# V rows gathered 8 tokens by 16 picks at a time and summed with 32-column weight blocks

## What is computed

```python
def block_fn(hb):                       # 128 tokens, four times
    q = (hb @ peer_wq).reshape(B, Q_BLOCK, PEER_HEADS, 2, PEER_HALF)
    s = jnp.einsum('bqhpd,hpnd->bqhpn', q, peer_subkeys).astype(jnp.float32)
    vals, idx = lax.top_k(s, PEER_TOPK)
    ...
    top_s, pos = lax.top_k(combo, PEER_TOPK)
    expert = jnp.take_along_axis(ids, pos, axis=-1)        # 128 tokens x 8 heads x 16 picks
    g = jax.nn.softmax(top_s, axis=-1).astype(hb.dtype)
    u_sel = peer_u[expert]
    a = jax.nn.gelu(jnp.einsum('bqhkd,bqd->bqhk', u_sel, hb))
    v_sel = peer_v[expert]
    return jnp.einsum('bqhk,bqhkd->bqd', g * a, v_sel)
```

## Time and profile before

| what | value |
|---|---|
| device time, median of 3 runs | 3902.87 us (3900.05 to 3913.13) |
| span of the profiled execution, first to last instruction | 3781.4 us |
| what lies around the span, by the median | 121.5 us |
| retrieval, first gather issued to last sum | 514 us to 1884 us of the span |
| gathers | 512 of U, 512 of V, 512 KB each |

### The profile page before, as it was taken

How to read it: one execution, slowest core, us unless ns; L and a number is a source line. 1 busy time by engine, 2 the same in 40 slices (tenths; PEclk the granted TensorE clock), 3 DMA queues, 4 the chain that set the end, 5 groups by cost and what they waited for, 6 DMA issues and landing times. The chain is left out here.

```text
span 3781.4 us, 35208 instructions
## 1 busy us (share of the span) xinstructions
PE 3188.5 (84%) x11752; PEld 1996.0 (53%) x11752; DVE 2418.9 (64%) x4629; ACT 1404.0 (37%) x2228; POOL 1168.3 (31%) x1095
## 2 busy tenths in 40 slices
PE   8988798887777777777788988997799999598878
PEld 4655543332222222222366876875688888465556
DVE  4866457666766776677576446445688888644444
ACT  2324312222222222222243323333588888534443
POOL 0000047777777777777600000000122222000000
PEclk9988799999999999999998988998899999799888
DMA  8322069999999999999932210134799999521101
GB/s 274 109 84 78 24 241 400 397 380 404 407 404 374 407 407 408 408 403 400 357 109 56 79 38 14 51 89 156 267 367 376 370 372 373 179 62 45 28 28 56
DMA packets 420694, 896.23 MB, mean 237 GB/s; under 512 B 37793, under 2 KB 178593, under 8 KB 419874
## 3 DMA queue, kind: packets, MB, share of 16 engines
q0 software_dynamic: 157728, 549.55, 37.1%
q1 hardware_dynamic: 262786, 344.41, 26.9%
HBM read 891.73 MB, written 27.27 MB: 243 GB/s over the span
## 5 line engine op out<-in xcount | busy, mean ns | idle before, releaser
L268 PE MATMUL peer_acc<-peer_vbuf,peer_diag 128*128 128x512 f32 x2016 | 981.3, 613 | 295.6 <-DMA peer_vbuf<-in_peer_v,peer_experts 209.9
L441 DVE CUSTOM_DVE_ANT_0 peer_junk<-peer_ubuf,firsts_h 128x1024 f32<-128x1024 f32 x512 | 626.6, 1225 | 385.3 <-DMA peer_ubuf<-in_peer_u,peer_experts 347.7
L268 PEld LDWEIGHTS peer_acc<-peer_vbuf,peer_diag 128*128 128x128 f32 x2016 | 351.3, 191 | 914.5 <-issue 472.3
L208 POOL DMA_INDIRECT peer_ubuf<-in_peer_u,peer_experts x512 | 526.5, 1028 | 672.7 <-DVE peer_experts L412 513.6
L219 POOL DMA_INDIRECT peer_vbuf<-in_peer_v,peer_experts x512 | 517.7, 1011 | 156.1 <-issue 120.1
L326 ACT ACTIVATE peer_diag<-all_consts,peer_weights 128x128 f32<-128x128 f32 x504 | 191.9, 398 | 800.5 <-PE peer_acc L268 730.6
L3029 DVE TENSOR_TENSOR slotted_low<-slotted_raw,slotted_high 128x2048 fp32r<-128x2048 f32 x192 | 434.1, 2288 | 66.0 <-ACT slotted_high L2978 66.0
L2978 ACT ACTIVATE slotted_high<-slotted_raw 128x2048 fp32r<-128x2048 f32 x192 | 365.5, 1920 | 63.6 <-PE slotted_h L2935 51.3
L2802 POOL MEMSET slotted_xg<- 128x4096 f32 x1 | 3.5, 3512 | 748.4 <-POOLq L60 748.4
L2935 PE MATMUL slotted_h<-slotted_high,slotted_xT_high 128*128 128x512 f32 x512 | 205.1, 401 | 6.2 <-DVE slotted_low L3029 4.1
L2935 PE MATMUL slotted_h<-slotted_high,slotted_xT_low 128*128 128x512 f32 x512 | 201.6, 394 | 0.0
(11 more groups left out here) (748 smaller groups left out, 5811.0 us busy)
## 6 DMA issues: line engine op xcount, KB each, us to landing
slotted_raw<-in_moe_w SPq DMA_DIRECT2D x192, 1024.0 KB, 8.4
mixers_raw<-in_w_in SPq DMA_DIRECT2D x56, 512.0 KB, 3.8
firsts_ada_raw<-in_w_ada SPq DMA_DIRECT2D x64, 256.0 KB, 2.7
third_raw<-in_w_in SPq DMA_DIRECT2D x30, 512.0 KB, 3.7
firsts_raw<-in_w_in SPq DMA_DIRECT2D x28, 512.0 KB, 4.1
firsts_ada_first<-in_w_ada SPq DMA_DIRECT2D x8, 1024.0 KB, 13.3
ffn_w_raw<-in_peer_wq SPq DMA_DIRECT2D x16, 512.0 KB, 7.5
peer_ubuf<-in_peer_u,peer_experts POOLq DMA_INDIRECT x512, 6.9
```

The lines of the kernel that those rows point to most:

```text
L208: pool.indirect_dma_start(ubuf[:, n % R, :], None, A["peer_u"], bass.IndirectOffsetOnAxis(ap=experts[:, t, m:m + 1], axis=0))\
L268: mm = nc.tensor.matmul(acc[t % 2][j][:, :], diag[:, q % 4, :], vbuf[:, n % R, j * BANK:(j + 1) * BANK], start=(m == 0), stop=(m == E - 1 ...
L441: nc.vector.tensor_tensor_reduce(junk[:, n % 2, :], ubuf[:, n % R, :], h2[:, t, :], 1.0, 0.0, ALU.mult, ALU.add, act_in[:, t, m:m + 1]).th ...
```

## The change

The rows of V are fetched in another grouping. Before, one gather held pick i of all 128 tokens. Now one gather holds all 16 picks of 8 tokens: partition 16 j + k is pick k of token 8 c + j, for the column c of a table `v_rows` of row numbers. Sixteen gathers a head, as before, and the same 2048 rows.

- **DVE** writes the picks of a head 8 times side by side (`ids`, 128 x 128). **PE** turns them (`turn_picks`, a matmul with the identity, in the middle of the V sums of the head before). DVE then masks and sums the turned picks to `v_rows` (`rows_of_v`: three operations, at the end of each head's pass), and POOL's first V gather of the head waits for that (`v_chosen`).
- The weights go the same way: `weigh` writes them 8 times, PE turns them (`turn_weights`), and `spread` on DVE (after dot 2 of the next head) makes of them 16 blocks of 32 columns, `spread_w`, in one operation.
- **PE** adds two gathers at a time (`add_rows`): for each a matmul of 128 x 32 weights by 512 columns into one 32-row quarter of the PSUM bank; gathers n and n+1 go to different quarters. As many matmuls as before.
- ACT's diagonals are gone. The dot product writes its products over `ubuf`, not into `junk`. The last head is summed by PE alone. One of four score banks becomes the bank for turning; a small table `own_rows` is loaded.

```diff
                 def gather_v(n):
-                    t, m = place(n)
-                    i = n - R - (G - 1) * PT
-                    if i >= 0 and i % 2:
-                        pool.wait_ge(v_summed, i // 2 + 1)
-                    elif n >= R:
-                        pool.wait_ge(added, n - R + 1 if i < 0 else n - R + 1 - i // 2)
+                    g, i = divmod(n, PT)
+                    if i == 0:
+                        pool.wait_ge(v_chosen, g + 1)
+                    if n >= R:
+                        pool.wait_ge(added, n - R + 1)
                     pool.indirect_dma_start(vbuf[:, n % R, :], None, A["peer_v"],
-                                            bass.IndirectOffsetOnAxis(ap=experts[:, t, m:m + 1], axis=0))\
+                                            bass.IndirectOffsetOnAxis(ap=v_rows[:, g % 2, column_of(i):column_of(i) + 1], axis=0))\
                         .then_inc(v_in[n % R], 16)
...
+                def turn_picks(g):
+                    pe.wait_ge(chosen, g + 1)
+                    if g >= 2:
+                        pe.wait_ge(v_chosen, g - 1)
+                    nc.tensor.matmul(turn_bank[:, tile(g % 2)], ids[:, g % 2, :], C["ident"], start=True, stop=True)\
+                      .then_inc(picks_turned, 1)
...
+                def add_rows(n0):
+                    g, i0 = divmod(n0, PT)
+                    t, h = divmod(g, PH)
+                    if i0 == 0:
+                        pe.wait_ge(weights_spread, g + 1)
+                    for n in (n0, n0 + 1):
+                        pe.wait_ge(v_in[n % R], 16 * (n // R + 1))
                     for j in range(2):
-                        mm = nc.tensor.matmul(acc[t % 2][j][:, :], diag[:, q % 4, :], vbuf[:, n % R, j * BANK:(j + 1) * BANK],
-                                              start=(m == 0), stop=(m == E - 1 or n == G * PT - 2))
-                    mm.then_inc(added, 1)
+                        for n in (n0, n0 + 1):
+                            i = n % PT
+                            rows32 = slice(32 * quarter_of(i), 32 * quarter_of(i) + 32)
+                            mm = nc.tensor.matmul(acc[t % 2][j][rows32, :], spread_w[:, g % 2, column_of(i), :],
+                                                  vbuf[:, n % R, j * BANK:(j + 1) * BANK],
+                                                  start=(h == 0 and i < 4), stop=(h == PH - 1 and i >= PT - 4))
+                            if j == 1:
+                                mm.then_inc(added, 1)
...
+                def rows_of_v(g):
+                    dve.wait_ge(picks_turned, g + 1)
+                    if g == 0:
+                        dve.wait_ge(own_in, 16)
+                    chain(nc.vector.tensor_tensor(picked[:, :, :], turn_bank[:, tile(g % 2)].rearrange("p (i j) -> p i j", i=PT),
+                                                  own8.unsqueeze(1).broadcast_to([P, PT, 8]), ALU.mult))
+                    chain(nc.vector.reduce_sum(v_rows_f[:, :], picked[:, :, :], AX))
+                    if g >= 2:
+                        dve.wait_ge(v_in[R - 1], 16 * (PT // R) * (g - 1))
+                    nc.vector.tensor_copy(v_rows[:, g % 2, :], v_rows_f[:, :]).then_inc(v_chosen, 1)
+
+                def spread(g):
+                    dve.wait_ge(weights_turned, g + 1)
+                    if g >= 2:
+                        dve.wait_ge(added, PT * (g - 1))
+                    nc.vector.tensor_tensor(
+                        spread_w[:, g % 2].rearrange("p (q r) c -> p q r c", q=4),
+                        turn_bank[:, tile(2 + g % 2)].rearrange("p (q c) -> p q c", q=4).unsqueeze(2).broadcast_to([P, 4, 4, 32]),
+                        own32.rearrange("p (r c) -> p r c", r=4).unsqueeze(1).broadcast_to([P, 4, 4, 32]), ALU.mult)\
+                      .then_inc(weights_spread, 1)
...
                         dot(g * PT + i)
                         if g and i == 0:
                             weigh(g - 1)
+                        if g and i == 2:
+                            spread(g - 1)
...
                     finish(coming)
+                    rows_of_v(g)
...
                 weigh(G - 1)
-                last_closed()
+                spread(G - 1)
+                collect(NT - 1)
+                dve.wait_ge(stored, 2 * NT)
+                finish(opened(NT - 1))
```

More of the change, by code:

```diff
@@ L160, in retrieval @@
         vbuf = st.sb("vbuf", [P, R, D])
-        junk = st.sb("junk", [P, 2, D])
         act_in = st.sb("act_in", [P, NT, E])
-        diag = st.sb("diag", [P, 4, P])
-        banks = [st.ps(f"s{i}") for i in range(4)]
+        v_rows, picked = st.sb("v_rows", [P, 2, PT], U32), st.sb("picked", [P, PT, 8])
+        own = st.sb("own", [P, 8 + P])
+        own8, own32 = own[:, 0:8], own[:, 8:8 + P]
+        v_rows_f, spread_w = st.sb("v_rows_f", [P, PT]), st.sb("spread_w", [P, 2, PT, 32])
+        score_banks, turn_bank = [st.ps(f"s{i}") for i in range(3)], st.ps("turn")
         acc = [[st.ps(f"acc{i}{j}") for j in range(2)] for i in range(2)]
@@ L172, in retrieval, with score_bank, quarter_of, column_of @@
         dotted, gelued, softened, weighed = st.sem("dotted"), st.sem("gelued"), st.sem("softened"), st.sem("weighed")
-        diagonal, added, stored, gate_in = st.sem("diagonal"), st.sem("added"), st.sem("stored"), st.sem("gate_in")
-        v_summed = st.sem("v_summed")
+        added, stored, gate_in = st.sem("added"), st.sem("stored"), st.sem("gate_in")
+        picks_turned, v_chosen, weights_turned, weights_spread = (st.sem(n) for n in ("picks_turned", "v_chosen", "weights_turned",
+                                                                                     "weights_spread"))
+        own_in = st.sem("own_in")
         def place(n):
             return n // E, n % E
[L179 to L183, removed]
+        def score_bank(q):
+            return score_banks[q % 3]
+        def quarter_of(i):
+            return i % 4
+        def column_of(i):
+            return 4 * (i % 4) + i // 4
+        def eight_times(rows):
+            return rows.unsqueeze(1).broadcast_to([P, 8, PT])
         def head(g):
@@ L198, in _ @@
                         sp.dma_start(skT[:, :, :], A["subkeys_T"]).then_inc(sk_in, 16)
+                        sp.dma_start(own[:, :], A["own_rows"]).then_inc(own_in, 16)
                 sp.wait_ge(scored, PH + 4 * (NT - 1))
@@ L279, in _ @@
                     per = len(steps) // KD
-                    for i in range(PT):
-                        add_row(h * PT + i)
-                        for step in steps[i * per:(i + 1) * per]:
+                    turn_weights(h)
+                    for i in range(0, PT, 2):
+                        add_rows(h * PT + i)
+                        if i == PT // 2:
+                            turn_picks(h + 1)
+                        for step in steps[i * per:(i + 2) * per]:
                             product(*step)
@@ L290, in _ @@
                         pe.wait_ge(stored, 2 * (t - 1))
[L291 to L294, removed]
+                    for g in range(t * PH, (t + 1) * PH):
+                        turn_weights(g)
+                        for i in range(0, PT, 2):
+                            add_rows(g * PT + i)
+                            if i == PT // 2 and g + 1 < G:
+                                turn_picks(g + 1)
+                        if g == t * PH + PH // 2 and t + 1 < NT:
                             later_scores(t + 1)
@@ L315, in gelu @@
                       .then_inc(gelued, 1)
[L317 to L327, removed]
                 def query_moved(m):
```

79 lines of the change are left out of this document (34 added, 45 removed).

## The result

The changed kernel takes 4000.04 us in the median of 4 runs (3991.27 to 4011.77). The kernel before, timed with it, took 3904.03 us (3900.05 to 3913.13), so the ratio is **1.0239, 95% interval 1.022 to 1.0258**: 96 us slower, where +110 was predicted. Timed again with the first group of experiments, the same two kernels took 3967.68 and 3771.49 us: **ratio 1.0531, 196 us**. There both have a trace (changed_again and base_again), so the prediction's steps are judged on those two.

The account below looks back on a forecast made before the run. DMA was taken as the bound. A loss of 3.10 us a head times 31 (96), start +7.5 and end +6.6 make 110 us: span 3781.4 + 110 = 3891.5, with 121.5 around it 4013 us; range for 8 in 10, 3972 to 4058.

Parts of the forecast that it names:

- DMA is the bound: Retrieval heads: the DMA queue is never empty, 1.32 us a gather, while POOL needs only 1.24.
- L + 1.15 + c + w - 3 d: Loss a head, 3.10 us: landing L, dot 1.15, rows_of_v c, POOL's restart w, less three gathers d of 1.32.
- c: DVE's rows_of_v at the end of a head's pass: three small operations with gaps, 0.80 us, at most 1.3.
- w: On POOL, from the end of the cast that releases it to its next gather: 0.29 us.
- start: Head 0's V gathers wait for its last dot product, going out at 549.5 in place of 542.00: +7.5 us.
- The end, +6.6: Last head's V sums: PE alone takes 8 pairs of 3.44 us without overlap, 37.4 us in place of 30.8.
- Nothing for ACT, DVE and PE: ACT's dropped diagonals gain nothing; DVE's about 2 us more a head and PE's new matmuls stay hidden.
- 121.5 us around the span: Time outside the profiled span, added to the predicted span of 3891.5 to give 4013 us.
- quick refill: Rival at the stop: refilling the queue costs only 3.7 us, loss 2.0 a head, total 3979 us; chance 0.12.
- Slower transfers by the new grouping: Rival in the V gathers: regularly spaced rows move at 371 GB/s, 48 us more, about 4060; chance 0.08.
- PE as the bound: Rival in the heads: PE at 1.2 GHz takes 55 us a head without overlap, +300 us, about 4310; chance 0.06.
- Not slower: Rival at the stop: the queue covers POOL's stop, 3917 us, or 3902 with start hidden and quarters overlapping; chance 0.04.

Follow-up runs that it names:

- wait_only: Kernel before plus one wait: a head's first V gather waits for that head's last dot product; 3964.97 us, 1.0527 of the kernel before.
- v_one_late: Changed kernel with every V gather one place later in POOL's order; 1.0357 of the kernel before.
- v_three_late: Changed kernel with every V gather three places later in POOL's order; 1.0186 of the kernel before.
- rows_at_12: Changed kernel with one line moved: V's rows made behind dot product 12 of the head, not the last; 3790.29 us, 1.0042 of the kernel before.
- changed_no_dots: Changed kernel with dot products left out, DVE multiplying one element a token, good for time alone; 3879.49 us, 1.0273 of the kernel before.
- sums_on_act: Changed kernel with picks turned earlier, V's rows made behind dot 8, DVE only multiplying and ACT adding up; 1.0101 of the kernel before.

## Why the prediction was right, and by what

The direction, the place and the look of the stop were right, and 4013 stood 13 us from 4000. The largest term behind it was not, and that the number came out is luck: in the first group of experiments the change costs 196 us, where the sum says 110. The sizes are set against those two.

**The bound.** "DMA is the bound", with POOL's 1.24 us a gather below DMA's 1.32, took POOL's gather from the median, 0.94. The mean is 1.02, with the 0.30 between two 1.32: in base_again POOL is never idle over 0.31 us in heads 8 to 30. So POOL has no reserve out of which to make good a stop. In the kernel before the transfers keep the same pace (41.55 us a head, where POOL's gathers weren't held, against 41.62), and which of the two is the limit there stays open. In the changed kernel it is POOL: it issues a gather every 1.36 us, and without held gathers the transfers keep 1.30. That POOL never waits elsewhere can be added up. A head should be 32 gathers of the mean, 31 gaps of 0.30, and the stop (or a 32nd gap):

| kernel | mean gather | stop, mean | added up | measured head |
|---|---|---|---|---|
| before (base_again) | 1.023 | 0.30 | 42.3 | 42.4 |
| wait_only | 1.066 | 4.43 | 47.8 | 47.9 |
| changed_again | 1.051 | 5.2 | 48.1 | 48.2 |
| v_one_late | 1.060 | 2.54 | 45.8 | 45.8 |
| v_three_late | 1.069 | 0.38 | 43.9 | 43.9 |
| rows_at_12 | 1.021 | 0.33 | 42.3 | 42.4 |
| changed_no_dots | 0.943 | 5.81 | 45.3 | 45.4 |

**The loss a head, the term that was mis-sized:** "L + 1.15 + c + w - 3 d" with L = 4.82, 3.1 us. L was the landing in an empty queue, on the ground that the transfers would catch up behind POOL. They don't: over heads 8 to 30 U gather 1, the first behind a stop, lands 5.6 us after its issue, U gather 3 6.4 and U gather 15 6.5 (6.9 is the median of the earlier trace rows), because the queue fills again. With 6.53 from U gather 15's issue to its dot, and 2.24 from the dot's start to V gather 0, the stop costs 6.53 + 2.24 - 3 x 1.32 = 4.8 us. A second part, 0.9, the prediction put at nothing: gathers held by dots, 32 x (1.051 - 1.023). Together 5.7, where 3.1 stood and 5.8 were measured, 180 us over 31 heads for 96. The same sum with five gathers in place of three gives v_one_late 2.2 + 1.2 = 3.4 (measured 3.4). Why the dots hold more gathers isn't shown. In heads 8 to 30 of base_again 44 of 735 gathers start 0.1 to 0.9 us into a dot, in changed_again 127; but v_three_late, which doesn't stop in these heads, has 132, and rows_at_12 54.

**c, w, start:** 0.81, 0.28 and +8.1 us (540.94 to 549.02), against 0.80, 0.29 and +7.5. Right; so is the 2.24 from the dot to V gather 0.

**The end, +6.6:** +0.5 (30.8 to 31.3 us). Here the sum took the wrong side: the quarters do overlap, 1.91 us a pair. The rule of the Trainium skill, "TensorE: Matmul & The Clock Gate", Part 3, gave this term as about nothing, and the trace agrees with it.

**Nothing for ACT, DVE and PE:** right on these traces. Start, heads and end make 8.1 + 180.5 + 0.5 = 189 of the 196 us, and rows_at_12 has all these edits and heads as long as before. The rest lies behind the retrieval, where no edit is; that part takes 1883 to 1897 us from trace to trace. In the first trace of the changed kernel POOL did stand for V buffers, 32 us as shown above, against the sign "POOL never waits over a us for PE".

**121.5 us around the span:** wrong. Every trace since has 1.8. So the trace shown ahead of the prediction was, by that 1.8, of an execution of some 3783 us, like those of the three groups, and the runs of 3904 were slower ones. The forecast hit because two errors met: the sum was put on 3904 with a head's loss of 3.1 us, and where before takes 3904 the whole change cost 96. Why the first measurement has 133 us more for the kernel before and 32 more for the changed one stays open, for no trace of a run of 3904 exists. For the changed kernel the 40.8 us more of that trace all lie in the heads. A queue that is slower by itself would have less to lose in a stop, but that is only argued.

**Rivals.** The quick refill is refuted: U gather 1, the first of U behind a stop, takes 5.6 us to its dot, at the least 5.1, not 3.7. V gather 0 itself, which goes out first, lands 4.4 us after its issue. The Trainium skill, "DMA: Bandwidth & Descriptors", Anatomy of one DMA, gave 3.2 us for it by an estimate, and no landing here agrees: the shortest of all traces that have landings is 3.9 (sums_on_act). Slower transfers by the new grouping: 409 GB/s in rows_at_12. PE as the bound: the clock did fall, to 0.67 to 0.79 in the heads; in changed_again and rows_at_12 it cost nothing that shows, and for the first trace it stays open. "Not slower" didn't come.

## What to carry to other kernels

When an engine issues gathers back to back, add up its row (mean duration, not median, plus the gaps) and compare it with the stretch before calling the transfers the only bound: if it fills the stretch, that engine has no reserve, and here every stop of it was lost in full. Price a new wait on the landing of the last gather with the landing time of the busy queue, and count how many gathers are issued between the two. Here the cure was to compute the waited-for value three dots earlier, one moved line, and it gave back 179 us of 196 (rows_at_12 is still 17 over the kernel before).

## What the runs showed of the hardware

- A gather's issue on POOL is held while a DVE instruction of 128x1024 with two inputs in SBUF runs: it ends 0.88 us after that instruction, up to 1.97 us in place of 0.94 (base_again, and sums_on_act for a plain product).
- The first gather into an emptied queue is followed by a ramp: in the mean of heads 8 to 30, 142, 299 and 371 GB/s in the first three stretches of 4 us (changed_again), without dots 166, 315 and 369 (changed_no_dots).
- Four-byte matmuls of 32 columns into different quarters overlap in pairs: eight in 1.91 us, where four of 128 columns take 1.96, both at a granted clock of 1.00.
